# A 288/256 split of 544 token columns, laid end to end across a PSUM bank border

## Time and profile before

| | |
|---|---|
| median of 3 runs | 2458.89 us (2456.26 to 2461.06) |
| span of the profiled execution | 2458.2 us; no time of its own is given beside the span |
| PE busy | 2418.5 us, 98% |
| DVE, ACT, POOL busy | 1094.6, 786.4, 376.0 us (45%, 32%, 15%) |
| granted TensorE clock | full in every one of the 40 slices |
| DMA | 78 GB/s of HBM traffic over the span |

### The profile page before, as it was taken

The page is one execution under the profiler, slowest core; times in us unless marked ns, Lnnn a source line. Parts: engine busy times, 40 slices in busy tenths (PEclk is TensorE's granted clock), DMA queues, the critical chain, the costliest instruction groups (busy, mean ns, idle before and its releaser), DMA issues.

```text
span 2458.2 us, 45368 instructions
## 1 busy us (share of the span) xinstructions
PE 2418.5 (98%) x19160; PEld 2367.9 (96%) x19160; DVE 1094.6 (45%) x1429; ACT 786.4 (32%) x1006; POOL 376.0 (15%) x324
## 2 busy tenths in 40 slices
PE   7999999999999999999999999999999999999998
PEld 7999999988989999999999999999999899999998
DVE  5333322556574333322433332488655654333322
ACT  4333322333323222222322222355345543222222
POOL 2101000000042111000111100143033531011000
PEclk9999999999999999999999999999999999999999
DMA  3222223322102222222222222322200012222221
GB/s 125 86 85 91 89 81 99 103 80 90 67 17 97 86 85 85 81 95 82 88 96 90 85 77 95 95 72 78 79 29 1 10 44 86 88 96 90 82 92 53
DMA packets 191214, 193.67 MB, mean 79 GB/s; under 512 B 4811, under 2 KB 188495, under 8 KB 191082
## 3 DMA queue, kind: packets, MB, share of 16 engines
q1 hardware_dynamic: 178286, 181.64, 22.7%
q10 hardware_dynamic: 12162, 8.11, 1.2%
q0 software_dynamic: 640, 2.10, 0.3%
HBM read 185.73 MB, written 6.10 MB: 78 GB/s over the span
## 4 chain that ended last, share of the span: by engine, by line
PE 93%; DVE 4%; issue 1%; ACT 1%; POOL 0%; ACTq 0%; DMA 0%; DVEq 0%; POOLq 0%
PE ps L570 81%; PE ps L2519 1%; PE ps L2504 1%; PE ps L2650 1%; DVE wl L555 1%; PE ps L2492 1%; PE ps L1089 0%; PE ps L1557 0%; PE ps L1654 0%; PE ps L777 0%; PE ps L2544 0%; PE ps L2538 0%; PE ps L2550 0%; PE ps L2559 0%; PE ps L1705 0%
## 5 line engine op out<-in xcount | busy, mean ns | idle before, releaser
L570 PE MATMUL ps<-xh,wh 128*128 128x272 f32 x3776 | 792.3, 291 | 3.5 <-DVE wl L555 2.8
L570 PE MATMUL ps<-xh,wl 128*128 128x272 f32 x3776 | 780.9, 288 | 0.0
L570 PE MATMUL ps<-xl,wh 128*128 128x272 f32 x3776 | 780.6, 288 | 0.0
L555 DVE TENSOR_TENSOR wl<-raw,wh 128x2048 fp32r<-128x2048 f32 (+1 forms) x173 | 390.6, 2258 | 508.8 <-ACT wh L550 508.8
L570 PEld LDWEIGHTS ps<-xh,wh 128*128 128x128 f32 x3776 | 593.4, 189 | 16.4 <-issue 9.2
L570 PEld LDWEIGHTS ps<-xl,wh 128*128 128x128 f32 x3776 | 594.9, 189 | 0.0
L570 PEld LDWEIGHTS ps<-xh,wl 128*128 128x128 f32 x3776 | 591.8, 189 | 0.0
L550 ACT ACTIVATE wh<-raw 128x2048 fp32r<-128x2048 f32 (+1 forms) x173 | 323.2, 1868 | 329.1 <-PE ps L570 323.2
L570 PE MATMUL ps<-hh,wh 128*128 128x272 f32 x1408 | 291.2, 288 | 0.0
L570 PE MATMUL ps<-hh,wl 128*128 128x272 f32 x1408 | 290.6, 288 | 0.0
L570 PE MATMUL ps<-hl,wh 128*128 128x272 f32 x1408 | 290.5, 288 | 0.0
(11 more groups left out here) (431 smaller groups left out, 2202.4 us busy)
## 6 DMA issues: line engine op xcount, KB each, us to landing
raw<-ffn_w_in SPq DMA_DIRECT2D x88, 1024.0 KB, 5.1
raw<-ffn_w_out SPq DMA_DIRECT2D x32, 1024.0 KB, 5.2
raw<-odd_w_in SPq DMA_DIRECT2D x16, 1024.0 KB, 5.7
raw<-even_w_in SPq DMA_DIRECT2D x14, 1024.0 KB, 5.1
raw<-ffn_w_out SPq DMA_DIRECT2D x16, 768.0 KB, 4.9
raw<-even_w_out SPq DMA_DIRECT2D x4, 1024.0 KB, 5.3
raw<-odd_w_out SPq DMA_DIRECT2D x4, 1024.0 KB, 5.1
xnat<-x_prompt SPq DMA_DIRECT2D x2, 1024.0 KB, 8.6
```

Of the source, the lines that this page charges most:

```text
L555: nc.vector.tensor_tensor(wl[slot][:, 0:kt, :], raw[slot][:, 0:kt, :], wh[slot][:, 0:kt, :].bitcast(F32), ALU.subtract).then_inc(lo_done.s ...
L570: ins = nc.tensor.matmul(ps[:, 2 * pe_out + b, 0:TH], w, r[:, rk, b * TH:(b + 1) * TH], start=first and a == 0, stop=last and a == 2)
```

## The change

The halves become parts of 288 and 256 tokens. Part 0 is written at columns 224 to 511 of its bank, part 1 at columns 0 to 255 of the next bank. In the tensor ps the two then lie end to end, and readers see one run of 544 columns, from column 224 of the first bank. (`halves` still cuts that run in two of 272, as `two` does with the other operands; the cut now lies between neighbouring columns.) Every matmul over tokens changes its column ranges in this way; the readers use `halves` as before, and two reads that spelled out the banks use it now too (three more lines of the same kind on ACT and DVE are left out below). In `conv_tile` the two reads of prompt tokens become one of 512 columns; the read of the 32 sample tokens and the small copy stay.

```diff
-TH = T // 2
+TOKENS = (slice(0, 288), slice(288, T))
+PCOLS = (slice(224, 512), slice(0, T - 288))
+PAT = 224
...
-    def halves(slot):
-
-        return ps[:, 2 * slot:2 * slot + 2, 0:TH]
+    def halves(slot, rows=P):
+
+        flat = ps[0:rows, 2 * slot:2 * slot + 2, :].rearrange("p a n -> p (a n)")
+        return two(flat[:, PAT:PAT + T])
...
         for a, (w, r) in enumerate(((w_hi, rh), (w_hi, rl), (w_lo, rh))):
             for b in range(2):
-                ins = nc.tensor.matmul(ps[:, 2 * pe_out + b, 0:TH], w, r[:, rk, b * TH:(b + 1) * TH],
+                ins = nc.tensor.matmul(ps[:, 2 * pe_out + b, PCOLS[b]], w, r[:, rk, TOKENS[b]],
                                        start=first and a == 0, stop=last and a == 2)
...
             dve.wait_ge(tap0.sem, tap0.at(i - 1))
-            nc.vector.tensor_tensor(pre[c][:, 3:3 + TH], ps[:, 2 * p, 0:TH], rstd[:, 0:TH], ALU.mult)
-            nc.vector.tensor_tensor(pre[c][:, 3 + TH:3 + SEQ], ps[:, 2 * p + 1, 0:SEQ - TH], rstd[:, TH:SEQ], ALU.mult)
+            flat = ps[:, 2 * p:2 * p + 2, :].rearrange("p a n -> p (a n)")
+            nc.vector.tensor_tensor(pre[c][:, 3:3 + SEQ], flat[:, PAT:PAT + SEQ], rstd[:, 0:SEQ], ALU.mult)
             nc.vector.tensor_copy(pre[c][:, 3 + SEQ:6 + SEQ], cols[:, 7 * KT + 4 + 7 * i:7 * KT + 7 + 7 * i])
-            nc.vector.tensor_tensor(pre[c][:, 6 + SEQ:PADT], ps[:, 2 * p + 1, SEQ - TH:TH], rstd[:, SEQ:T], ALU.mult).then_inc(proj_out.sem, 1)
+            nc.vector.tensor_tensor(pre[c][:, 6 + SEQ:PADT], flat[:, PAT + SEQ:PAT + T], rstd[:, SEQ:T], ALU.mult).then_inc(proj_out.sem, 1)
```

More of the change, by code:

```diff
@@ L612, in stats_pe @@
         for b in range(2):
-            ins = nc.tensor.matmul(ps[:, 6 + b, 0:TH], ones[:], ssq[:, b * TH:(b + 1) * TH], start=True, stop=True)
+            ins = nc.tensor.matmul(ps[:, 6 + b, PCOLS[b]], ones[:], ssq[:, TOKENS[b]], start=True, stop=True)
         ins.then_inc(ssq_psum.sem, 1)
@@ L776, in hgrn_part @@
                     for a, (w, r) in enumerate(((w_hi, rh), (w_hi, rl), (w_lo, rh))):
-                        last = nc.tensor.matmul(ps[:, 2 * c + b, 0:TH], w, r[:, k, b * TH:(b + 1) * TH],
+                        last = nc.tensor.matmul(ps[:, 2 * c + b, PCOLS[b]], w, r[:, k, TOKENS[b]],
                                                 start=False, stop=k == KT - 1 and a == 2)
@@ L1171, in norm_sums @@
                 for b in range(2):
-                    ins = nc.tensor.matmul(ps[0:4, 4 + b, 0:TH], asel[:, h, :], att[:, 4 + h, b * TH:(b + 1) * TH],
+                    ins = nc.tensor.matmul(ps[0:4, 4 + b, PCOLS[b]], asel[:, h, :], att[:, 4 + h, TOKENS[b]],
                                            start=h == 0, stop=h == HEADS - 1)
@@ L1183, in norm_wide @@
             for b in range(2):
-                ins = nc.tensor.matmul(ps[:, 2 * (3 - h % 2) + b, 0:TH], pick[:, h:h + 1].broadcast_to([48, P]),
-                                       row_parts[:, b * TH:(b + 1) * TH], start=True, stop=True)
+                ins = nc.tensor.matmul(ps[:, 2 * (3 - h % 2) + b, PCOLS[b]], pick[:, h:h + 1].broadcast_to([48, P]),
+                                       row_parts[:, TOKENS[b]], start=True, stop=True)
             ins.then_inc(an_wide.sem, 1)
@@ L1228, in even_proj_act @@
                 act.wait_ge(an_psum.sem, an_psum.at(1))
-                nc.scalar.activation(two(an_row), ps[0:4, 4:6, 0:TH], ACT.Sqrt, scale=1.0 / P, bias=eps[0:4, 1:2]).then_inc(an_rms.sem, 1)
+                nc.scalar.activation(two(an_row), halves(2, 4), ACT.Sqrt, scale=1.0 / P, bias=eps[0:4, 1:2]).then_inc(an_rms.sem, 1)
                 attention_over(act)
@@ L1653, in sums @@
                     for a, part in enumerate((l2q, l2l)):
-                        ins = nc.tensor.matmul(ps[0:16, 6 + b, 0:TH], sel_r[:, i, :], part[i % 4][:, b * TH:(b + 1) * TH],
+                        ins = nc.tensor.matmul(ps[0:16, 6 + b, PCOLS[b]], sel_r[:, i, :], part[i % 4][:, TOKENS[b]],
                                                start=i == 0 and a == 0, stop=i == 15 and a == 1)
@@ L1669, in widen @@
             for b in range(2):
-                ins = nc.tensor.matmul(ps[:, 2 * side_banks(p) + b, 0:TH], pick[:, i:i + 1].broadcast_to([48, P]),
-                                       row_parts[:, b * TH:(b + 1) * TH], start=True, stop=True)
+                ins = nc.tensor.matmul(ps[:, 2 * side_banks(p) + b, PCOLS[b]], pick[:, i:i + 1].broadcast_to([48, P]),
+                                       row_parts[:, TOKENS[b]], start=True, stop=True)
             ins.then_inc(l2_wide.sem, 1)
@@ L1704, in odd_proj_pe @@
                     for k in range(KT):
-                        ins = nc.tensor.matmul(ps[0:16, 6 + b, 0:TH], wabg[:, k, :], x[:, k, b * TH:(b + 1) * TH],
+                        ins = nc.tensor.matmul(ps[0:16, 6 + b, PCOLS[b]], wabg[:, k, :], x[:, k, TOKENS[b]],
                                                start=k == 0, stop=k == KT - 1)
@@ L1756, in gates_dve_row @@
         dve.wait_ge(ab_psum.sem, ab_psum.at(1))
-        nc.vector.tensor_tensor(two(gate_row), ps[0:16, 6:8, 0:TH], two(rstd[0:16, :]), ALU.mult).then_inc(ab_row.sem, 1)
+        nc.vector.tensor_tensor(two(gate_row), halves(3, 16), two(rstd[0:16, :]), ALU.mult).then_inc(ab_row.sem, 1)
     def gates_dve_col(dve):
@@ L1916, in conv_act @@
                 act.wait_ge(l2_psum.sem, l2_psum.at(8))
-                nc.scalar.activation(two(l2r), ps[0:16, 6:8, 0:TH], ACT.Sqrt, scale=1.0, bias=eps[0:16, 0:1]).then_inc(l2_rt.sem, 1)
+                nc.scalar.activation(two(l2r), halves(3, 16), ACT.Sqrt, scale=1.0, bias=eps[0:16, 0:1]).then_inc(l2_rt.sem, 1)
             if v >= 13:
@@ L2649, in tile_half @@
                 for a, (w, r) in enumerate(((w_hi, mixh), (w_hi, dlo), (w_lo, mixh))):
-                    ins = nc.tensor.matmul(ps[:, 2 * (2 * q + c) + b, 0:TH], w, r[:, k, b * TH:(b + 1) * TH],
+                    ins = nc.tensor.matmul(ps[:, 2 * (2 * q + c) + b, PCOLS[b]], w, r[:, k, TOKENS[b]],
                                            start=k == 0 and a == 0, stop=k == KT - 1 and a == 2)
```

## The result

The changed kernel takes 2441.26 us, the median of four runs (2437.53 to 2443.74), where the kernel before takes 2459.43 (2456.26 to 2461.06). The ratio is 0.9924, with a 95% interval of 0.9910 to 0.9937: 18 us faster, outside the range that was given (2446 to 2476), and faster where no change was the forecast.

The account below looks back on a forecast made before the run. PE's pace was taken to bound the kernel, busy 98% of the span. Steps 0, readers 0, convolution -0.1 and L2650 +0.3 summed to +0.2 us on the 2458.9 median: 2459.0 us, range 2446 to 2476.

Parts of the forecast that it names:

- 2F + 544r: All 8,192 resized fp32r pairs: cost linear in columns, so 288 + 256 costs the same as 272 + 272; zero change.
- a floor: Rival at every mm3 pair: the short piece stays at about 125 ns; +6.7 ns a pair, +55 us, 2514 us; chance 8%.
- groups of 32 columns: Rival at the fp32r matmuls: columns fetched in 32s, so 272 costs as much as 288; -114 us, 2345 us; chance 6%.
- 0.3 ns each way: mm3 steps at 125.0 or 125.3 ns for no known reason; new widths may shift the pace, 5 us each way.
- faster, a shift of a few tenths: Case at the fp32r matmuls: costs stay linear but the pace lands a few tenths of a ns lower; chance 14%.
- the straight line: Fp32r steps linear in width through 256, 272 and 288 columns; 2451 to 2467 us; chance 83%.
- Readers: 280 DVE reads of 544 PSUM columns: one piece saves some 3 ns, hidden; zero, a bank crossing 0 to +1 us.
- Convolution: Two DVE reads become one of 512 columns, 826 to 688 ns, 3.3 us of DVE; hidden behind PE, taken as -0.1 us.
- Plain fp32: Matmuls of L1705, two cycles a column: linear in width by the same argument, so resizing them costs zero.
- The waits of PE: Sign that the forecast is right: PE's waits stay as they are, with none gone at the convolution.
- The slow form below 256 columns: Rival at the short piece: fp32r at full speed needs more than 256 columns; +797 us, 3256 us; chance 3%.
- The signs to look for: Profile checks: pairs at 250.0 to 251 ns if right; 3,168 mm3 matmuls in 375, 407 or 525 us if wrong.

Follow-up runs that it names:

- e4: New kernel without the encoder: 22 streams of 192 fp32r matmuls on PE alone, in mm3's order; 288 + 256 stepped at 124.2 ns, 272 + 272 at 125.3.
- e5: Against e4: 37 streams of 96 matmuls with other orders, starts, pitches, fewer weight columns; 288 + 256 took 123.9 ns in turn, 126.0 in blocks, 125.1 in threes.
- e11: The changed kernel with the two loops of mm3 turned, three long matmuls then three short; 2457.64 us, ratio 0.9987 to the kernel before.
- e7: Against e4: 38 streams of 96 matmuls with other starts and row pitches; at pitch 0, 288 + 256 stepped at 123.3 to 125.2 ns by start.
- e6: The changed kernel with three PSUM reads in the convolution as before (272, 240 and 32 columns); 2441.24 us.
- e3: The changed kernel with parts of 280 and 264 columns, end to end in PSUM; 2489.83 us, ratio 1.0123 to the kernel before.
- e8: The changed kernel with parts of 304 and 240 columns, end to end in PSUM; 2470.63 us, ratio 1.0045 to the kernel before.
- e9: Against e4: 39 streams of 96 matmuls, high and low parts in one buffer at varied distances; streams from equal places stepped at 123.4 or 125.0 ns.
- e12: Against e4: 34 streams of 96 matmuls at pitch 544, both parts moved by 4 to 60 columns; 288 + 256 took 124.1 ns moved by 32, otherwise 124.9 to 126.6.
- e13: Against e4: 68 streams of 96 matmuls, 288 + 256 at pitch 544, high and low parts moved separately; copies of one stream took 11.84 or 12.00 us.
- e10: The changed kernel with buffers xh, xl, hh and hl each beginning 64 bytes past a multiple of 128; 2450.03 us, ratio 0.9961 to the kernel before.

## Why the prediction was wrong

**The step that failed** is "with any fixed part F and any rate r, the pair costs 2F + 544r before and after". Fixed part and rate are there, about 6 ns and 0.44 ns a column in streams of one width (e4). But the sentence takes a matmul's step to be its own, and so puts the change of the pair at zero. It depends on its neighbours: 288 + 256 in turn, from the changed kernel's starts, steps at 123.9 where the line has 125.5, and with the same matmuls in threes or blocks it is back within 0.5 ns of the line (e5, e11). What the runs showed in place of the zero is 125.3 - 123.9 = 1.4 ns a matmul, 22 us of `mm3` in the trace and 18 us in the medians. I had asked for a bend in one matmul's cost over its width, and both bends that I priced (a floor, groups of 32 columns) were about that; neither shows between 256 and 288 columns. That the buffers lay where the mixture is cheap was luck: 16 columns further on it would have been 125.4 in a stream (L252 in e5), and about no change.

**What the trace of before had to say.** The 125.0 and 125.3 ns of the earlier trace rows were read as a small unknown, "0.3 ns each way". They were most likely two rhythms of one stream, the very mechanism: the streams of 272 + 272 from 0 and 272 at pitch 544 took 12.00 us in e5 (L180) and 12.03 in e7 (L320). Its size for another pair of widths was five times that, and nothing in the trace bounded it. The chance of 14% for "faster, a shift of a few tenths" had the right kind of cause with too small a size. The forecast's +-0.5 ns for the straight line should have been +-2 ns, the spread of the streams over places (123.3 to 126.8).

**The other steps.** Readers: 723 ns before and after, no effect of the bank border, as said. Convolution: 681 ns for 688, DVE 2.9 us lower for 3.3, nothing on the path (e6). L2653: +0.3 us foretold for its stretch up to the first read; 2015.04 - 1996.08 = 18.96 us became 1997.19 - 1977.80 = 19.39, so +0.4. L780: 7.73 us became 7.83, where zero was foretold. Plain fp32 (L1708): linear, 7.44 us both times. The waits of PE are as they were, 3.5 us for 3.2 at L573 and 2.7 at L780.

**The rivals.** Groups of 32 columns: no; the gain is a fifth of what they would give, and 280 + 264, nine groups each like 272 + 272, should have cost what that costs and is 2 ns a matmul dearer in e3. The floor: it exists at 111.6 ns (e4) and stays under the short piece, as rows 5 said. (Their 107 ns take in a short first step; from start to start the others are 111 to 112 ns apart.) It does bind for shorter pieces: 240 columns step at 112.8 in e5, 1.5 ns above the line, and with 304 on the line, 139.4 as an estimate, the mean is e8's 126.1. The slow form below 256 columns: no (e4); why L1670 takes two cycles a column wasn't tried. The signs to look for did their work: the chain of 3,168 matmuls, named as the judge, fell to 392.5 us where 396 to 398 would have been the forecast.

**What stays open**: what in PE or its reads makes the rhythms. Shown is on what they depend: the order, the starts modulo 64 columns of both sources, and the state before. Whether the weight reads take part is not shown. A row pitch of 576 columns, at which all rows would start alike, wasn't tried in the encoder; by e9 it could fall into either rhythm.

## What to carry to other kernels

Where one kind of matmul is five sixths of the time, half a ns in its step (8 us here) is worth a run: measure it in a stream of its own, in the order of the kernel and from its addresses, before arguing from columns and clocks. A stream of equal matmuls doesn't tell the step of a mixture, a stream of a mixture tells it only from the same starts (280 + 264 above), and a gain found so can hang on a buffer's start: after moving any buffer, read the length of a long stretch in the chain of waits again. An edit for the readers of a PSUM tile is worth nothing while they wait for TensorE.

## What was not expected of the hardware

- 288 + 256 columns in turn step at 123.9 ns a matmul, 280 + 264 at 127.2, 304 + 240 at 126.1, 272 + 272 at 125.3, all for the same 544 columns at the encoder's buffers (e3, e8); elsewhere 288 + 256 steps at 123.3 to 126.7 and 280 + 264 at 124.3 to 126.8 (e5, e7, e12, e13).
- One stream of matmuls on one set of addresses runs at 123.4 or at 125.0 ns each, keeps its pace for as long as it is left alone (3,120 matmuls in e10, six streams in e9), and changes it after a foreign stream.
- fp32r on 128 rows has no slow form between 192 and 512 columns. Its rate from 256 columns on is 0.44 ns a column, not the 0.417 of one column per cycle of 2.4 GHz, and 128 weight columns set a floor of 111.6 ns (e4, e5).
